# Moving the start of one-core buffers by 32 to 96 bytes: three small buffers widened at the front of the on-chip memory

## The chip, the cores and the metric

The kernel runs on one core of a Trainium2 chip. The metric is the device time of one execution in microseconds (us). Three runs of the kernel before gave 1700.7, 1705.86 and 1712.12 us; the median is 1705.86 us. The engines are named as in the profile: PE is TensorE (with PEld for its weight loads), DVE is VectorE, ACT is ScalarE, POOL is GpSimd, SP is SyncE, which here only issues transfers.

## The reference

Two transformer blocks are applied to one sequence of 256 tokens with 1024 features, all in float32. Cut to what matters:

```
first_block:  mod = silu(c) @ w_ada + b_ada                 # 1024 x 6144
              h = norm(x)*(1+scale1)+shift1 ; proj = h @ w_in
              attention over the 64 best keys of each query (chosen by an index score), short convolution
              x += gate1 * (mix @ w_out)
              h2 = norm(x)*(1+scale2)+shift2
              x += gate2 * peer_ffn(h2)
peer_ffn:     for each token: 8 heads x 16 experts of 16384 are chosen by product keys
              a = gelu(u[expert] . h2) ; sum of g*a * v[expert]    # u and v rows of 1024 floats
second_block: two feed-forwards of width 2816, retention with a context of 256 tokens,
              a Fourier branch, merge, final norm                  # weights of 1024 x 5632, 2816 x 1024, ...
```

The weights are much larger than the data: 538.50 MB pass through the DMA engines in one execution. About half of that is the expert rows: 256 tokens x 128 experts x 8 KB.

## The kernel before

**Memory.** Everything on the chip lies in buffers of 128 partitions. The helper `sb(name, width)` in `program` takes `width` words of 4 bytes from each partition, and buffers are laid one behind another in the order of the calls; the allocator starts each on a multiple of 32 bytes. In the compiled program the starts are, in bytes within a partition:

```
buffer      start    width in bytes   start modulo 64
ring        16512    65536            0
x_t         82048     8192            0
h_t         90240     8192            0
prm         98432      968            0
early       99424     3200            32
ones       102624      512            32
mod1       103136      192            32
mod2       103328      576            32
cols       103904      544            32
silu       104448      528            0
rstd       104992     1024            32
arena      106016   110592            32
small      216608    10336            32
ids        226944     1024            0
idx_stage  227968       64            0
found      228032     1024            0
spare      229056      128            0
```

**What lies where.** `ring` has four homes (slots 0 to 3) of 16 KB per partition for weight slabs. `arena` is 27648 words: two more homes for slabs (`extra`, at words 11264 and 23552), the eight buffers `rows` for expert rows (8 KB per partition each, from word 11264), homes of early modulation slabs (`spare_slab`), and most of the activations. `small` has activations and tables; its first 2048 words hold the upper half (`h_hi`) of the split activations, while the lower half (`h_lo`) is `h_t` read as float32r. `prm` has the small parameters, `early` constants, `cols` and `silu` columns of scales and of the modulation's input. `ids` has the chosen experts' numbers, `idx_stage` the 16 of them that are being fetched. `twin` gives a buffer a second name for float32r (`arena_r`, `small_r`, `h_t_r`, `ring_r`); `extra_float` and `upper` are names for parts of `arena`.

**Order of the work.** Each engine has its own written-out list, and semaphores tie the lists.
- SP (L1308 to L1364) loads `prm`, `x_t`, and then slab after slab in the order of `slab_order`, each as soon as its home is free (L1350); spare slabs of the modulation go to `arena` (L1313).
- POOL fetches expert rows. `one_round` (L1389 to L1405) copies 8 numbers from `ids` to `idx_stage` (L1395) and issues one indirect transfer for each (L1402), as soon as `row_open` finds one of the 8 buffers `rows` free. One transfer brings a row of 8 KB to each of 128 partitions.
- DVE takes the dot product of each fetched row (L2527, in `dot_batch`). The second half of the row is summed for the first 128 tokens by PE with diagonal weights (matmuls that read `small,arena`), for the last 128 tokens by DVE (L2538, in `sum_batch`) but for the last batches; after that the buffer is free.
- In the same stage PE does the context's feed-forward, with weights from `ring`. In the second block each weight piece is split in two float32r parts, the upper by ACT (L1455), the lower by DVE (L2016), and PE does three products of each; L518 is PE's matmul helper `mm`.

Of the kernel before, what the change touches and what calls it, by code (L numbers as in the profile page):

```python
# [90 lines left out]
def offsets(table):  # L91
    at, out = 0, {}
    for name, width in table:
        out[name] = (at, width)
        at += width
    return out, at


PARAM_AT, PARAM_W = offsets(PARAMS)
# [123 lines left out]
def program(nc, dram, out):  # L223
# [14 lines left out]
    with ExitStack() as ctx:  # L238
        def sb(name, width, dt=F32):
            return ctx.enter_context(nc.sbuf_tensor(name, [P, width], dt))  # L240
# [8 lines left out]
        def sem(name):  # L249
            if name not in sems:  # L250
                sems[name] = ctx.enter_context(nc.semaphore(name))
            return sems[name]
# [3 lines left out]
        x_t = sb("x_t", KD * L)[:].rearrange("p (k t) -> p k t", k=KD)  # L256
        h_words, h_words_r = twin("h_t", KD * L)
        h_t, h_lo = (t[:].rearrange("p (k t) -> p k t", k=KD) for t in (h_words, h_words_r))
        prm = sb("prm", PARAM_W)
        early = sb("early", EARLY_W)  # L260
        place = nc.alloc_sbuf_tensor_at("place", [P, SLOTS], U32, offset=nc.sbuf_base - 4 * EARLY_W + 4 * EARLY_AT["causal"][0])
        ones = sb("ones", P)
        mod1 = sb("mod1", 48)
        mod2 = sb("mod2", 144)
        mod2_v = mod2[:].rearrange("p (m k s) -> p m k s", m=9, s=2)
        cols = sb("cols", 136)
        silu = sb("silu", 132)
        rstd = sb("rstd", L)
        arena, arena_r = twin("arena", 27648)

# [148 lines left out]
        def home_of(n, ring_of):  # L419

            slot, words = slots[n][0], slabs[n][2]
            if slot >= RING:
                return extra[slot - RING][0 if ring_of is ring else 1][:, 0:words]
            return ring_of[:, slot * SLAB:slot * SLAB + words]
# [31 lines left out]
        def emptied(name):  # L456

            _, who, count = groups[index[name]]
            return drained[who], count
# [7 lines left out]
        def _(pe):  # L467
# [157 lines left out]
            def pair_by_block(o, need, hi, lo, name, order):  # L625

                two = [next_piece(j) for j in range(2)]
                for n, k in enumerate(order):
                    if k in need:
                        pe.wait_ge(*need.pop(k))  # L630
                    last = [three(o[:, j * L:(j + 1) * L], w_hi[:, k, :], w_lo[:, k, :], hi(k), lo[:, k, :],
                                  n == j == 0, n == KD - 1 and j == 1) for j, (_, w_hi, w_lo) in enumerate(two)]
                piece_end(last[0])
                piece_end(last[1], name)

            def split_feature(tag, count, hi, lo, who, kb=KD, need=None, start=0, order=range(KD)):


                need = need or {}
                for n in range(start, start + count):  # L640
                    o = begin(f"{tag}{n}", who)
                    if len(need) == KD and kb == KD:
                        pair_by_block(o, need, hi, lo, f"{tag}{n}", order)
                        continue
                    for j in range(2):
                        for part in range(kb // KD):
                            (k0, k1, _, _), w_hi, w_lo = next_piece()
                            for k in range(k0, k1):
                                if k in need:
                                    pe.wait_ge(*need.pop(k))  # L650
                                last = three(o[:, j * L:(j + 1) * L], w_hi[:, k - k0, :], w_lo[:, k - k0, :],
                                             hi(k), lo[:, k, :], k == 0, k == kb - 1)
                            ends = j == 1 and part == kb // KD - 1
                            piece_end(last, f"{tag}{n}" if ends else None)
# [653 lines left out]
        @block.sync  # L1308
        def _(sp):
            def load_spare(m):  # L1310

                home = SPARE_HOME[m][0]
                sp.dma_start(spare_slab[home], dram["w_ada_2"][MODS[m][1]]).then_inc(sem(f"spare_landed{home}"), 16)  # L1313

            sp.dma_start(prm[:], dram["params"]).then_inc(sem("params"), 16)
            sp.dma_start(x_t.rearrange("p k t -> p (k t)"), dram["x"]).then_inc(sem("x_landed"), 16)
            for n, (name, i, words) in enumerate(slabs):
                slot, _, replaced = slots[n]
                if slabs[n][:2] == ("w_ada", 5):
                    sp.wait_ge(group_done, index["ss_n1"] + 1)  # L1320
                    load_spare(12)
                if slabs[n][:2] == ("peer_wq", 1):
                    sp.wait_ge(*spare_read[12])
                    load_spare(14)
                    sp.wait_ge(*piece_read[first_pieces - 1])
                    sp.dma_start(subkeys.rearrange("p h n -> p (h n)"), dram["subkeys"][0]).then_inc(sem("subkeys"), 16)
                    sp.wait_ge(group_done, index["pt0_1"] + 1)
                    load_spare(15)
                if slabs[n][:2] == ("peer_wq", 2):
                    sp.wait_ge(sem("y_conv"), 1)  # L1330
                    sp.wait_ge(group_done, index["pv3"] + 1)
                    load_spare(16)
                    load_spare(17)
                    sp.wait_ge(*spare_read[14])
                    load_spare(19)
                    sp.wait_ge(*spare_read[15])
                    load_spare(18)
                    sp.wait_ge(*spare_read[16])
                    load_spare(20)
                if replaced is not None:  # L1340
                    sp.wait_ge(*slab_free[replaced])
                if slabs[n][:2] == MODS[LAST_ROWS[0]]:
                    sp.wait_ge(group_done, index["pr3"] + 1)
                if n == tail_at:
                    sp.wait_ge(row_landed[GBUF - 2], 16 * (NT * SLOTS // GBUF))
                if slot == RING and replaced is None:
                    sp.wait_ge(sem("row_free_dve"), GBUF + SLOTS - GBUF + 2)
                if slot == RING + 1 and replaced is None:
                    sp.wait_ge(group_done, index["yt1_1"] + 1)
                sp.dma_start(home_of(n, ring), dram[name][i]).then_inc(landed[slot], 16)  # L1350
                if n == 0:
                    sp.dma_start(early[:], dram["early"]).then_inc(sem("early_landed"), 16)
                if n == tail_at + LATE_AFTER:
                    sp.wait_ge(sem("experts_added"), 1)
                    at = 0
                    for dst, w, s in ((late_decay, LATE_DECAY, "p m t i -> p (m t i)"), (dft, LATE_DFT, "p a s c -> p (a s c)"),
                                      (rope, LATE_ROPE, "p a t -> p (a t)"), (late_xi, LATE_XI, "p a t -> p (a t)")):
                        sp.dma_start(dst.rearrange(s), dram["late"][:, at:at + w]).then_inc(sem("late"), 16)
                        at += w
            for i in range(2):  # L1360
                sp.wait_ge(sem("out_ready"), i + 1)
                sp.dma_start(out[:, 4 * i * L:(4 * i + 4) * L],
                             h_t[:, 4 * i:4 * i + 4, :].rearrange("p k t -> p (k t)")).then_inc(sem("stored"), 16)
            sp.wait_ge(sem("stored"), 16 * 2)  # L1364
# [1395 lines left out]
```

## Time and profile before

| what | value |
|---|---|
| median of 3 runs | 1705.86 us |
| the profiled execution, its own time | 1705.73 us |
| its span in the trace | 1703.8 us |
| instructions | 29036 |
| PE busy | 1627.5 us (96%) |
| DVE busy | 1167.1 us (68%) |
| ACT busy | 660.5 us (39%) |
| POOL busy | 389.6 us (23%) |
| moved by DMA | 538.50 MB, mean 316 GB/s |
| granted PE clock, mean | 0.987 |

The span is the time between the first and the last instruction of the profile; the device time of the same execution is 1.9 us longer. A busy share is an average over stages: PE counts as busy also where a matmul waits for its operands, and DMA is full in one part of the span and half idle in another, so the slices and windows have to be read and not the mean.

### The profile page before, as it was taken

How to read it: one execution, taken by the hardware profiler on the slowest of the kernel's cores; microseconds unless marked ns; L12 is line 12 of the kernel's file. 1: busy time of each engine (PE TensorE's matmuls, PEld its weight loads, DVE VectorE, ACT ScalarE, POOL GpSimd, SP SyncE). 2: the span in 40 equal slices, each digit the busy share in tenths (PEclk: the TensorE clock that was granted, in tenths of full speed). 3: DMA queues.
4: the chain of work that ended last, by engine and by line, in shares of the span. 5: the costliest groups of instructions: out<-in, count | busy, mean ns of one | idle time of the engine just before them, and what ended most of it. 6: DMA issues, size and time to landing. Idle time of an engine off the chain costs nothing.

```text
span 1703.8 us, 29036 instructions
## 1 busy us (share of the span) xinstructions
PE 1627.5 (96%) x11656; PEld 1464.0 (86%) x11656; DVE 1167.1 (68%) x1989; ACT 660.5 (39%) x1272; POOL 389.6 (23%) x317
## 2 busy tenths in 40 slices
PE   5999999988899899999998999999999999999997
PEld 3877889988899799998988567889998977989997
DVE  3675458778997677889788688564575456665554
ACT  3534133324433543433112158444434423444443
POOL 0553034434444434445343310000000000000000
PEclk9999999999999999999999999999999999999999
DMA  9868899999999999999999999865444522644442
GB/s 369 323 264 369 357 413 408 412 419 399 413 410 392 419 393 414 415 420 420 420 411 414 421 414 404 317 239 212 165 172 187 198 99 99 228 183 183 183 170 93
DMA packets 57732, 538.50 MB, mean 316 GB/s; under 512 B 6401, under 2 KB 6529, under 8 KB 7425
## 3 DMA queue, kind: packets, MB, share of 16 engines
q1 hardware_dynamic: 20592, 267.18, 39.5%
q0 software_dynamic: 37008, 269.50, 38.6%
q8 instruction: 92, 1.51, 0.4%
q14 instruction: 40, 0.32, 0.0%
HBM read 535.60 MB, written 1.05 MB: 315 GB/s over the span
## 4 chain that ended last, share of the span: by engine, by line
PE 62%; DMA 19%; DVE 10%; issue 6%; ACT 1%; POOL 1%; POOLq 0%; DVEq 0%; SPq 0%; ACTq 0%
PE psum L518 62%; DMA arena<-in_experts,idx_stage 16%; DVE arena L2538 4%; DVE arena L2527 1%; DMA ring<-in_w_ada 1%; POOL arena L1402 1%; DMA ring<-in_w_in 1%; DMA arena<-in_w_ada 1%; DMA extra_float<-in_w_ada 1%; DVE ring_r L2016 0%; POOL idx_stage L1395 0%; DVE arena L2649 0%; DVE small L2527 0%; DVE arena_r L2082 0%; ACT h_t L1832 0%
## 5 line engine op out<-in xcount | busy, mean ns | idle before, releaser
L2527 DVE CUSTOM_DVE_ANT_0 arena<-arena 128x1024 f32<-128x1024 f32 x256 | 313.8, 1226 | 133.5 <-DMA arena<-in_experts,idx_stage 127.4
L1402 POOL DMA_INDIRECT arena<-in_experts,idx_stage x256 | 303.8, 1187 | 365.7 <-DVE arena L2538 164.9
L2016 DVE TENSOR_TENSOR ring_r<-ring,ring_r 128x1024 fp32r<-128x1024 f32 (+1 forms) x200 | 240.7, 1214 | 197.0 <-ACT ring_r L1455 196.0
L518 PE MATMUL psum<-small_r,ring_r 128*128 128x256 f32 x1600 | 285.9, 283 | 3.4 <-DVE h_t_r L2097 3.4
L1455 ACT ACTIVATE ring_r<-ring 128x1024 fp32r<-128x1024 f32 (+1 forms) x200 | 208.2, 1048 | 170.4 <-PE psum L518 150.2
L518 PE MATMUL psum<-small,arena 128*128 128x128 f32 x2112 | 251.4, 280 | 22.0 <-ACT small L1858 21.7
L518 PEld LDWEIGHTS psum<-small,arena 128*128 128x128 f32 x2112 | 246.1, 196 | 25.9 <-ACT small L1858 23.0
L518 PEld LDWEIGHTS psum<-small_r,ring_r 128*128 128x128 f32 x1600 | 245.3, 189 | 5.4 <-issue 5.2
L518 PE MATMUL psum<-h_t,ring 128*128 128x256 f32 (+1 forms) x1360 | 248.1, 341 | 1.2 <-DMA ring<-in_w_in 1.2
L518 PEld LDWEIGHTS psum<-h_t,ring 128*128 128x128 f32 x1360 | 219.3, 191 | 21.9 <-DMA ring<-in_w_in 1.4
L518 PE MATMUL psum<-h_t_r,ring_r 128*128 128x256 f32 x800 | 223.8, 280 | 0.0
L518 PE MATMUL psum<-arena_r,ring_r 128*128 128x256 f32 x1488 | 211.6, 284 | 2.8 <-DVE arena_r L2082 2.8
L1920 ACT ACTIVATE small<-small 128x2 f32<-128x2 f32 x127 | 25.8, 203 | 463.9 <-DVE small L2527 463.8
L518 PEld LDWEIGHTS psum<-arena_r,ring_r 128*128 128x128 f32 x1488 | 192.9, 191 | 3.2 <-DVE arena_r L2082 3.2
L2538 DVE SCALAR_TENSOR_TENSOR arena<-arena,small 128x1024 f32<-128x1024 f32 x123 | 158.1, 1285 | 5.7 <-ACT small L1851 1.3
L518 PEld LDWEIGHTS psum<-h_t_r,ring_r 128*128 128x128 f32 x800 | 151.1, 189 | 0.1
L518 PE MATMUL psum<-arena,ring 128*128 128x128 f32 (+1 forms) x916 | 141.8, 316 | 0.0
L518 PEld LDWEIGHTS psum<-arena,ring 128*128 128x128 f32 x916 | 130.4, 192 | 10.7 <-issue 1.7
L518 PEld LDWEIGHTS psum<-ring 128*128 128x128 f32 x1056 | 122.9, 195 | 3.4 <-DVE ring L2478 1.9
L518 PE MATMUL psum<-ring 128*128 128x128 f32 x1056 | 123.2, 279 | 1.9 <-DVE ring L2478 1.7
L518 PE MATMUL psum<-ring_r,small_r 128*128 128x512 f32 x272 | 90.1, 399 | 0.8 <-DVE ring_r L2016 0.8
L518 PE MATMUL psum<-arena_r,upper 128*128 128x256 f32 x384 | 73.9, 295 | 9.9 <-DVE ring_r L2016 5.6
(281 smaller groups left out, 1687.6 us busy)
## 6 DMA issues: line engine op xcount, KB each, us to landing
ring<-in_w_in SPq DMA_DIRECT2D x31, 2048.0 KB, 8.6
ring<-in_w_ffn SPq DMA_DIRECT2D x29, 2048.0 KB, 11.2
ring<-in_w_ada SPq DMA_DIRECT2D x18, 2048.0 KB, 9.5
ring<-in_w_ffn SPq DMA_DIRECT2D x23, 1408.0 KB, 7.4
arena<-in_w_ada SPq DMA_DIRECT2D x8, 2048.0 KB, 16.4
ring<-in_w_out SPq DMA_DIRECT2D x4, 2048.0 KB, 9.3
ring<-in_peer_wq SPq DMA_DIRECT2D x4, 2048.0 KB, 10.3
extra_float<-in_w_ffn SPq DMA_DIRECT2D x4, 2048.0 KB, 12.5
```

The source lines that it names most:

```text
L518: return nc.tensor.matmul(o, a, b, start=first, stop=last)
L1402: nc.gpsimd.indirect_dma_start(rows[slot % GBUF], None, dram["experts"], bass.IndirectOffsetOnAxis(ap=idx_stage[:, slot:slot + 1], axis=0) ...
L1455: nc.scalar.activation(upper(i), whole(i, ring), ACT.Copy).then_inc(hi_made, 1)
L1920: nc.scalar.activation(acts[:, n % 8, :], dots[:, n % 8, :], ACT.Gelu_apprx_tanh).then_inc(sem("gelus"), 1)
L2016: nc.vector.tensor_tensor(whole(i, ring_r), whole(i, ring), upper(i).bitcast(F32), ALU.subtract).then_inc(lo_made, 1)
L2527: step(nc.vector.tensor_tensor_reduce(u, u, h2[:, n // PER_TILE, :], 1.0, 0.0, ALU.mult, ALU.add, dots[:, n % 8, s:s + 1]), sem("dots"))
L2538: ins = STT(y_sum, row, weight, y_sum, ALU.mult, ALU.add)
```

## The change

`prm` is widened from 242 to 256 words, `cols` from 136 to 144, `silu` from 132 to 144. The load of `prm` names its first 242 words, so it moves what it moved before. Every other instruction stays and addresses the same words of the same buffers, whose starts are now these:

```
buffer      start    modulo 64      moved by
early       99456    0              32
ones ... cols        0              32
silu       104512    0              64
rstd       105088    0              96
arena      106112    0              96
small      216704    0              96
ids        227040    32             96
idx_stage  228064    32             96
found      228128    32             96
spare      229152    32             96
```

`ring`, `x_t`, `h_t` and `prm` keep their starts. `small` is 2584 words, 161.5 times 64 bytes, so the four buffers behind it come to lie between two multiples of 64.

```
-        prm = sb("prm", PARAM_W)
+        prm = sb("prm", PARAM_W + -PARAM_W % 16)
         early = sb("early", EARLY_W)
...
-        cols = sb("cols", 136)
-        silu = sb("silu", 132)
+        cols = sb("cols", 144)
+        silu = sb("silu", 144)
         rstd = sb("rstd", L)
         arena, arena_r = twin("arena", 27648)
...
-            sp.dma_start(prm[:], dram["params"]).then_inc(sem("params"), 16)
+            sp.dma_start(prm[:, 0:PARAM_W], dram["params"]).then_inc(sem("params"), 16)
```

## Rows read from the trace of the kernel before

**Rows 1.** The page's slices of the span: clock, DMA share and rate.

```profile
PEclk9999999999999999999999999999999999999999
DMA  9868899999999999999999999865444522644442
GB/s 369 323 264 369 357 413 408 412 419 399 413 410 392 419 393 414 415 420 420 420 411 414 421 414 404 317 239 212 165 172 187 198 99 99 228 183 183 183 170 93
```

**Rows 2.** The page's chain that ended last, by engine.

```profile
PE 62%; DMA 19%; DVE 10%; issue 6%; ACT 1%; POOL 1%; POOLq 0%; DVEq 0%; SPq 0%; ACTq 0%
```

**Rows 3.** Who waited for whom: us in total, times, longest us.

```profile
POOL arena L1402 <- DVE arena L2538: 164.9, 45, 12.2
...
POOL arena L1402 <- PE psum L518: 133.3, 71, 10.2
DVE arena L2527 <- DMA arena<-in_experts,idx_stage: 127.4, 80, 6.2
```

**Rows 4.** Windows: stretch, us, each engine's busy us, clock, DMA share, GB/s.

```profile
5.00:30.00 25.00, 15.03 (x74) 10.62 (x75) 13.05 (x32) 11.43 (x15) 0.00 (x0) 0.88 1.01 432
7.00:19.00 12.00, 10.21 (x48) 5.85 (x48) 4.88 (x18) 4.29 (x6) 0.00 (x0) 1.00 1.00 427
110.00:115.00 5.00, 5.00 (x49) 4.86 (x49) 0.19 (x1) 0.00 (x0) 1.44 (x1) 1.00 1.00 423
...
178.00:200.00 22.00, 22.00 (x195) 18.89 (x194) 5.95 (x17) 5.08 (x14) 0.00 (x0) 1.00 1.01 427
213.00:1005.00 792.00, 757.09 (x5185) 689.84 (x5185) 631.69 (x1212) 259.76 (x705) 328.33 (x288) 0.98 1.00 412
937.00:980.00 43.00, 43.00 (x123) 23.24 (x122) 28.48 (x36) 6.30 (x23) 15.49 (x14) 1.00 1.01 422
```

**Rows 5.** SP's queue in time: start us, us, transfers issued in a row.

```profile
3.87 12.92 SPq L1350 DMA_DIRECT2D ring<-in_w_ada  x2
18.93 0.33 SPq L1350 DMA_DIRECT2D ring<-in_w_idx  x1
...
105.15 0.33 SPq L1350 DMA_DIRECT2D ring<-in_w_in  x1
...
166.47 25.21 SPq L1313 DMA_DIRECT2D arena<-in_w_ada  x5
```

**Rows 6.** The page's DMA issues: KB each, median us from issue to landing.

```profile
ring<-in_w_ada SPq DMA_DIRECT2D x18, 2048.0 KB, 9.5
...
arena<-in_w_ada SPq DMA_DIRECT2D x8, 2048.0 KB, 16.4
```

**Rows 7.** DVE and ACT, groups by form: busy us, mean ns, idle before.

```profile
L2016 DVE TENSOR_TENSOR ring_r<-ring,ring_r 128x1024 fp32r<-128x1024 f32 x192 | 233.1, 1224 | 188.2 <-ACT ring_r L1455 187.1
...
L2016 DVE TENSOR_TENSOR extra_float32r<-extra_float,ring_r 128x1024 fp32r<-128x1024 f32 x16 | 19.3, 1223 | 2.0 <-ACT ring_r L1455 1.9
...
L2082 DVE TENSOR_TENSOR arena_r<-arena,arena_r 128x1024 fp32r<-128x1024 f32 x4 | 4.9, 1224 | 1.3 <-ACT arena_r L1977 1.2
```

**Rows 8.** PE, groups by form, same columns.

```profile
L518 PE MATMUL psum<-small_r,ring_r 128*128 128x256 f32 x1600 | 285.9, 283 | 3.4 <-DVE h_t_r L2097 3.4
L518 PE MATMUL psum<-h_t,ring 128*128 128x256 f32 x848 | 186.5, 380 | 1.2 <-DMA ring<-in_w_in 1.2
L518 PE MATMUL psum<-arena,ring 128*128 128x256 f32 x352 | 77.4, 380 | 0.0
```

**Rows 9.** PE matmuls of 1500 to 1690 us by tile: min/median/max ns.

```profile
L518 PE MATMUL psum<-small_r,ring_r x704: 275/282/375, 1506.3 to 1631.8; 128*128 128x256 f32 x176
L518 PE MATMUL psum<-arena_r,ring_r x495: 277/280/283, 1632.0 to 1689.9; 128*128 128x256 f32 x165
L518 PE MATMUL psum<-h_t_r,ring_r x352: 276/277/284, 1506.4 to 1631.7; 128*128 128x256 f32 x176
```

**Rows 10.** POOL's indirect transfers and index copies by tile: min/median/max ns.

```profile
L1402 POOL DMA_INDIRECT arena<-in_experts,idx_stage x256: 932/1004/1931, 213.6 to 988.3; - x128
L1395 POOL COPY idx_stage<-ids x32: 187/924/1208, 212.4 to 966.0; 128x8 uint32 x26, 128x8 uint32<-128x8 uint32 x6
```

**Rows 11.** DVE's clearing of `silu` by tile: min/median/max ns.

```profile
L2190 DVE MEMSET silu<- x1: 168/168/168, 0.8 to 0.8; 128x132 f32 x1
```

**Rows 12.** The page's issue row of the expert rows (256 x 1 MB).

```profile
arena<-in_experts,idx_stage POOLq DMA_INDIRECT x256, 11.6
```

## The prediction

> **What bounds the kernel now.** The slices of the span come first, because the change moves addresses and nothing else, and an address can matter only where a resource that uses it is full. They show two parts [rows 1]. Up to about 213 us the DMA share wavers between 0.6 and 1; from there to about 1060 us it is full in every slice, at 392 to 421 GB/s; from 1100 us on it is mostly about half, at 93 to 240 GB/s. The clock digits show nothing but nines: PE's granted clock is near its full level of 2.4 GHz throughout, so the clock is no lever here.
>
> The chain that ended last gives PE 62%, DMA 19% and DVE 10% [rows 2]. The waits tell how DMA and DVE are tied in the full part: DVE waits 127.4 us for expert rows, and POOL waits 164.9 us for DVE's sum and 133.3 us for PE to free a row buffer [rows 3]. It is a loop over eight buffers. A transfer takes 11.6 us at the median from issue to landing [rows 12], though 1 MB at the stage's 412 GB/s [rows 4] needs only 2.5 us: the rest is queueing, so POOL's and SP's issues are well ahead of the engines that move the bytes. From 213 to 1005 us the windows have DMA at 1.00 and PE busy for 757 of 792 us. So a faster or slower DMA write to `arena` would show there, and a slower PE read would show everywhere else.
>
> **The change part by part.** It removes no instruction and adds none. Three questions of cost are left, one for each kind of access, and one small term.
>
> *The clearing of `silu`* covers 144 words in place of 132. The memset took 168 ns for 132 [rows 11]; 12 more at 168/132 = 1.3 ns each are at most 15 ns. It runs at 0.8 us, when DVE would otherwise wait for the first loads. Without that cover it would cost the 15 ns. I take 0. The load of `prm` moves the same 242 words to the same place: 0.
>
> *DMA writes to `arena`* (all 256 MB of expert rows, 16 MB of early modulation slabs, the `extra` slabs) start 32 bytes past a multiple of 64 now and will start on one. The trace holds both kinds side by side, since `ring` and `x_t` already start on multiples of 64. From 7 to 19 us the queue carries the slabs issued to `ring` and the early small loads [rows 5], at 427 GB/s and share 1.00; from 178 to 200 us it carries modulation slabs to `arena`, at 427 GB/s and share 1.01 [rows 4]. A second stretch with `ring` alone, 110 to 115 us, behind the issue at 105.15, has 423. The same size of row, the same queue, the same rate: the start makes no difference that this trace can show. One row seems to speak the other way: a modulation slab takes 9.5 us to land in `ring` and 16.4 us in `arena` [rows 6]. But five of the eight `arena` slabs were issued close together, from 166.47 to 191.7 us [rows 5], and at 427 GB/s each needs 2.1 MB / 427 = 4.9 us, so 16.4 us is the time to stand behind two others and not a slower write. Value taken: 0. The ends: a gain if `arena` in the full part (422 GB/s in its quietest window) rose to the best `ring` window, 432 [rows 4], 2.3% of 792 us = 18 us; a loss if it fell from 427 to the worst, 423, 0.9% of 792 us = 7 us. Both are too large even so, as part of those 792 us is bounded by PE.
>
> The Trainium skill ("DMA: Bandwidth & Descriptors", How a descriptor splits into AXI transactions) knows no step at 64 bytes but one at 256: a transfer that starts off such a boundary pays for the bytes below its start. It speaks against this change, for by the addresses a row starts 32 past a boundary before and 128 past it after: 8 + 248 + 1 = 257 beats against 8 + 248 + 4 = 260. By that rule my sum would be 1.2% of the full part, +9 us, an estimate from the page. The trace does not agree, since `ring`, which lies 128 past a boundary, would have to be slower than `arena`, and the two windows above are equal.
>
> *DVE and ACT* work on both kinds of addresses in the same operation. The lower part of a piece of 128x1024 takes 1224 ns in `ring`, 1223 ns in `extra` and 1224 ns from `arena` to `arena` [rows 7]. Value 0; the end is 1 ns x 256 dot products, 0.3 us, on either side.
>
> *PE* reads its moving operand from `h_t` or from `arena`: 380 ns both, over 848 and 352 matmuls [rows 8]. In float32r one pair differs: 282 ns at the median from `small_r` (off 64) and 277 from `h_t_r` (on 64) [rows 9]. This looks like a price of the address. But in the second feed-forward's other half both parts come from `arena_r`, off 64 all of them, and yet their times span 277 to 283 ns with a median of 280. A third of the matmuls takes the lower part there too. So the 5 ns go with the place in the triple of products, not with the buffer. Value 0. The end, if the address were the cause: 5 ns x 1600 matmuls [rows 8] = 8 us of gain, and about as much again for `arena_r` at half the difference or less; I put 12 us.
>
> *`ids` and `idx_stage`* lose the multiple of 64. POOL's issue of an indirect transfer takes 932 ns at least and 1004 at the median, the copy of 8 numbers 924 [rows 10]. The numbers in slots 8 to 15 of `idx_stage` lie 32 bytes on already, and half of the 256 issues use them; the median is only 72 ns above the least. If every issue paid 72 ns more it would be 18 us on POOL, which is busy for 328 of the stage's 792 us [rows 4] and whose issues land 11.6 us later from queueing. The queue's depth hides it; without that cover it would be the 18 us. Value 0.
>
> **The sum** is 0 against the profiled execution, 1705.73 us, a span of 1703.8 and 1.9 us around it. The median of the runs, 1705.86, is 0.1 us above it. The three runs lie 11 us apart (0.7%), which is why I take 1% as the least that can be told from no change. Forecast 1705.
>
> **The rivals.** *Faster: the write to an aligned `arena` is quicker.* For it: the full part has 412 GB/s on average and 422 at its quietest, `ring` alone reached 432. Against it: the 427 and 427 of the direct comparison, and that the full part's writes are mixed with instruction and index traffic. Gain 9 us (422 to 427) to 18 us (to 432), so 1688 to 1697. Chance 9%.
>
> *Faster: PE's reads.* The 5 ns of above, a gain of about 12 us, 1694. Against it the spread of the `arena_r` matmuls. Chance 3%.
>
> *Slower: rows that start 128 past a boundary of 256.* It decides in the full part, where DMA is at 1.00, and only while DMA's rate and not PE sets the pace. Priced from rows it is the step from 427 to 423 GB/s, 7 us, time 1713. For it: the second `ring` window. Against it: the first. Chance 7%. The page's rule named above would make it 9 us.
>
> *The change does not do what it says.* The four buffers of indices end up off the 64, and something there matters: POOL's fetch, which reads one number per partition from `idx_stage`. It would need the buffers' loop to run short of issues: up to 18 us, 1724; partly hidden, 1710. Chance 3%.
>
> **How the numbers follow.** The forecast has 78%. Of the two gains, 12% together, 7 points exceed 1% (17 us) when I allow that a price can be larger than the rows' ends; of the two losses, 10%, 5 points do. The same: 100 - 7 - 5 = 88%. The range reaches from 1694, where the gains are at their middle, to 1715, past the loss from the 256 boundary, and includes the 1701 to 1712 of the kernel's own scatter.
>
> **What would show it.** Equal instruction counts and the same chain. In windows with DMA at 1.00 between 213 and 1005 us, the rate stays near 412 GB/s, and the last expert row is issued within a few us of 988 [rows 10]. The writes' rival would show a stage that ends some 9 to 18 us earlier at a higher rate; PE's rival, `small_r` matmuls at 277 ns; the 256 rival, 5 GB/s less in the windows of slabs to `arena`; the index rival, POOL's least time above 932 ns. I am wrong if DMA gains in the mixed traffic what it does not show in the lone stretches.

## The result, and the profile after

The change makes the kernel slower by a little: 1711.23 us median against 1705.30, a ratio of 1.0034 with a 95% interval of 1.0023 to 1.0045. The profiled execution has a span of 1709.4 us against 1703.8, so the trace holds 5.6 us of it. The order of the instructions is the same on every engine, 29036 of them; the one shape that differs is that of the clearing of `silu`, 128x144 for 128x132.

The page after, its busy times:

```profile
PE 1633.1 (96%) x11656; PEld 1470.1 (86%) x11656; DVE 1170.0 (68%) x1989; ACT 660.2 (39%) x1272; POOL 386.8 (23%) x317
```

PE is busy for 1633.1 us, 5.6 more than before. The windows of the changed kernel (columns as in [rows 4]), three of those of [rows 4] first, then three in the second block:

```profile
7.00:19.00 12.00, 9.52 (x44) 5.85 (x48) 4.89 (x18) 5.07 (x5) 0.00 (x0) 1.00 1.00 427
...
178.00:200.00 22.00, 22.00 (x195) 18.89 (x194) 5.95 (x17) 4.64 (x13) 0.00 (x0) 1.00 1.01 429
213.00:1005.00 792.00, 758.17 (x5195) 689.21 (x5188) 632.58 (x1219) 260.52 (x706) 325.20 (x289) 0.99 1.00 412
...
1240.00:1275.00 35.00, 35.00 (x294) 35.00 (x293) 26.00 (x33) 13.47 (x14) 0.00 (x0) 1.00 0.48 181
...
1510.00:1620.00 110.00, 110.00 (x918) 109.94 (x917) 61.06 (x65) 52.12 (x62) 0.00 (x0) 1.00 0.49 186
1640.00:1685.00 45.00, 45.00 (x378) 45.00 (x377) 24.53 (x28) 20.85 (x30) 0.00 (x0) 1.00 0.48 174
```

The same three windows of the kernel before:

```profile
1240.00:1275.00 35.00, 35.00 (x300) 35.00 (x299) 26.60 (x33) 13.20 (x13) 0.00 (x0) 1.00 0.48 181
...
1510.00:1620.00 110.00, 110.00 (x936) 109.97 (x935) 61.23 (x62) 53.07 (x62) 0.00 (x0) 1.00 0.49 186
1640.00:1685.00 45.00, 45.00 (x386) 45.00 (x385) 23.57 (x27) 21.96 (x30) 0.00 (x0) 1.00 0.44 161
```

The first thing to see is what did not move. The expert rows' stage runs at 412 GB/s before and after, the slabs to `arena` at 427 and 429. POOL's indirect transfers end where they ended (compare [rows 10]):

```profile
L1402 POOL DMA_INDIRECT arena<-in_experts,idx_stage x256: 932/1060/1978, 214.9 to 988.7; - x128
```

The last is issued at 988.7 us for 988.3. So at most 0.4 us of the 5.6 come from the part in which DMA is full; the rest comes after it.

The second thing is the count beside PE. In the second block's windows PE is busy for the whole of them, before and after, and its share says nothing. But fewer matmuls fit: 918 for 936, 378 for 386, 294 for 300. A matmul lasts some 280 ns by its record and overlaps its neighbours, so a window counts also those that started up to 0.28 us before it, and the pace, the time from the start of one matmul to the start of the next, is (window + 0.28) / count: 110.28/936 = 117.8 ns before, 110.28/918 = 120.1 after; 45.28/386 = 117.3 before, 45.28/378 = 119.8 after. The durations show it only weakly, 283 to 284 ns for `small_r` (compare [rows 8]):

```profile
L518 PE MATMUL psum<-small_r,ring_r 128*128 128x256 f32 x1600 | 290.2, 284 | 3.4 <-DVE h_t_r L2097 3.4
L518 PE MATMUL psum<-h_t_r,ring_r 128*128 128x256 f32 x800 | 226.5, 283 | 0.0
L518 PE MATMUL psum<-arena_r,ring_r 128*128 128x256 f32 x1488 | 214.5, 286 | 2.7 <-DVE arena_r L2082 2.7
```

The same groups had busy times of 285.9, 223.8 and 211.6 us before, so these three grew by 9.9 us; others shrank: the 272 matmuls with 512 columns from `ring_r` against `small_r` from 90.1 to 89.1, those within `ring` from 123.2 to 121.8, those from `small,arena` from 251.4 to 250.6. The row of `h_t_r` is the telling one: `h_t` and `ring` have not moved by a byte, and its matmuls are slower all the same.

### The profile page after: what moved, and what is told of

It reads as the page before. It is cut to its first block, busy times and chain, and to the rows that moved or that the text cites. A ratio compares the mean times of both kernels' runs of the same rounds, so it can differ in the third digit from the quotient of the medians.

```text
span 1709.4 us, 29036 instructions
## 1 busy us (share of the span) xinstructions
PE 1633.1 (96%) x11656; PEld 1470.1 (86%) x11656; DVE 1170.0 (68%) x1989; ACT 660.2 (39%) x1272; POOL 386.8 (23%) x317
## 4 chain that ended last, share of the span: by engine, by line
PE 61%; DMA 19%; DVE 10%; issue 6%; ACT 2%; POOL 1%; POOLq 0%; DVEq 0%; SPq 0%; ACTq 0%
PE psum L518 61%; DMA arena<-in_experts,idx_stage 16%; DVE arena L2538 4%; DVE arena L2527 1%; DMA ring<-in_w_ada 1%; DMA ring<-in_w_in 1%; POOL arena L1402 1%; DMA arena<-in_w_ada 1%; DMA extra_float<-in_w_ada 1%; DVE ring_r L2016 0%; DVE small L2527 0%; DVE arena L2649 0%; DVE arena_r L2082 0%; ACT h_t L1832 0%; ACT L1920 0%
## 5 line engine op out<-in xcount | busy, mean ns | idle before, releaser
L2527 DVE CUSTOM_DVE_ANT_0 arena<-arena 128x1024 f32<-128x1024 f32 x256 | 313.8, 1226 | 133.5 <-DMA arena<-in_experts,idx_stage 127.2
L518 PE MATMUL psum<-small_r,ring_r 128*128 128x256 f32 x1600 | 290.2, 284 | 3.4 <-DVE h_t_r L2097 3.4
L518 PE MATMUL psum<-small,arena 128*128 128x128 f32 x2112 | 250.6, 279 | 20.8 <-ACT small L1858 20.6
L518 PEld LDWEIGHTS psum<-small_r,ring_r 128*128 128x128 f32 x1600 | 250.6, 192 | 5.5 <-issue 5.2
L518 PE MATMUL psum<-ring 128*128 128x128 f32 x1056 | 121.8, 277 | 1.6 <-DVE ring L2478 1.6
L518 PE MATMUL psum<-ring_r,small_r 128*128 128x512 f32 x272 | 89.1, 395 | 0.8 <-DVE ring_r L2016 0.8
```

The source lines that it names most:

```text
L518: return nc.tensor.matmul(o, a, b, start=first, stop=last)
L2527: step(nc.vector.tensor_tensor_reduce(u, u, h2[:, n // PER_TILE, :], 1.0, 0.0, ALU.mult, ALU.add, dots[:, n % 8, s:s + 1]), sem("dots"))
```

## The experiments

All experiments on the full kernel change the layout of the memory alone, except two at the end. The quantity that they turned out to be about is the distance from the start of `ring` (weights) to the start of `arena` or `small` (moving operand), modulo 256 bytes: 160 before (106016 - 16512 = 89504 = 349 x 256 + 160), 0 after (89600 = 350 x 256). `h_t` is at 0 in both. The first four expectations name a window of 42.6 us (364 matmuls before, 357 after); the two windows from 1510 and from 1640 us, each in one kind of work, have taken its place. Each kernel was timed against the kernel before on the same chip.

**Arena, and what lies behind it, moved by 32 bytes** (`small` and the index buffers move with it).

```
         rstd = sb("rstd", L)
+        gap = sb("gap", 8)
```

> The kernel before with one unused buffer of 8 words put between rstd and arena: arena and small move by 32 bytes onto a multiple of 64, ids to spare move with them off it, everything in front of them stays. Theory PE: a float32r matmul of 256 columns paces at 120 ns when its moving operand lies on a multiple of 64 (or at the same place in 64 as the weights) and at 117 ns when it lies 32 bytes off; the whole slowdown of the change comes from arena and small. It expects 1711 us, and 357 matmuls in a window of 42.6 us filled with them (364 before). Theory front: the slowdown comes from the small buffers in front (cols, silu, early, rstd): 1705 us and 364. Theory DMA (rows further behind a boundary of 256 bytes cost more; arena is now 64 behind one, 32 before the change, 128 after it): a third of the loss, 1707 us, with 364 matmuls in the window.

Measured: 1701.32 us, ratio 0.9974 (0.9959 to 0.9990). Faster, where one theory had 1711, another 1705, the third 1707. `arena` lies on a multiple of 64 here as in the changed kernel, and the pace of the matmuls from it is the quickest seen, 45.28/399 = 113.5 ns. So 64 is not the rule. The distance is 192. The index buffers lie off a multiple of 64 here as in the changed kernel, and the kernel is faster all the same: they are not the cause either.

```profile
1510.00:1620.00 110.00, 110.00 (x925) 110.00 (x924) 60.26 (x59) 51.91 (x60) 0.00 (x0) 1.00 0.49 186
1640.00:1685.00 45.00, 45.00 (x399) 45.00 (x398) 24.90 (x30) 22.08 (x30) 0.00 (x0) 1.00 0.45 161
```

**The changed kernel with the same gap** (distance 32).

> The changed kernel with the same unused buffer of 8 words between rstd and arena: the front stays on multiples of 64, arena and small go back to 32 bytes off (160 behind a boundary of 256). Theory PE: the loss is gone, 1705 us, 364 matmuls in the window. Theory front: 1711 us, 357. Theory DMA: at 160 behind a boundary no better than at 128, 1711 us or more, with 364 in the window.

Measured: 1704.26 us, ratio 0.9991 (0.9977 to 1.0005), 388 matmuls in the last window and 935 in the one before. The loss is gone with the front buffers still moved: it does not come from them, and it is not DMA's.

**Everything of the changed kernel moved by 32 bytes**, with one line ahead of `ring`:

```
+        shift = sb("shift", 8)
         ring, ring_r = twin("ring", RING * SLAB)
```

> The changed kernel with an unused buffer of 8 words in front of ring: every buffer of the change moves by 32 bytes, so the weights in ring and the moving operands in small, arena and h_t are all 32 off a multiple of 64. Two forms of theory PE part here. Absolute: the moving operand's own place in 64 counts; all are off, so 1705 us or a little less and 364 or more in the window. Relative: what counts is whether moving operand and weights lie at the same place in 64; they do, so 1711 us and 357.

Measured: 1709.06 us, ratio 1.0021 (1.0008 to 1.0034), still slow. `ring`, `h_t`, `arena` and `small` all lie 32 off a multiple of 64 now, and PE paces as in the changed kernel (the profiled execution took 1705.68 us):

```profile
1640.00:1685.00 45.00, 45.00 (x377) 45.00 (x377) 23.23 (x27) 21.25 (x29) 0.00 (x0) 1.00 0.42 158
```

The relative form of the theory holds: the distance counts, the place does not. This kernel and the one above it are the sharpest pair here: `arena`, `small` and the index buffers start at the same addresses in both (`arena` at 106144), and only `ring` and what lies between it and `arena` start 32 bytes further in this one. They take 1709.06 and 1704.26 us, so neither DMA's writes to `arena` nor the index buffers can be what separates them.

**The kernel before with the same line ahead of ring** (distance 160 again, `arena` on a multiple of 64).

> The kernel before with an unused buffer of 8 words in front of ring: ring and h_t come to lie 32 off a multiple of 64, arena and small on one. Weights and moving operands are 32 apart for arena and small, as before the change, but with the roles exchanged. Absolute: arena and small on 64 pace at 120 ns, so about 1710 us. Relative: 1705 us, 364 in the window.

Measured: 1705.39 us, ratio 0.9994 (0.9981 to 1.0008), as the relative form has it. The windows have 927 and 382, 118.9 and 118.5 ns, between before and after, where 936 and 386 were expected. The distance of 160 has two paces in these kernels, and the kernel before shows both by itself: from `arena`, 171 matmuls in the window from 1435 to 1455 us (20.28/171 = 118.6 ns) and the 386 of the last window (117.3).

**PE alone.** The kernel has the second block's pattern of matmuls on zeros, no other engine at work:

```
for k in range(3):
    mm(o, w_hi[k], hi[k]); mm(o, w_hi[k], lo[k]); mm(o, w_lo[k], hi[k])
```

> This kernel computes nothing of the reference: PE alone runs matmuls in the second block's pattern (of three, the first two with the same weights, the third with others; 256 columns of float32r) on zeros, 144 from each of 14 buffers that start 0, 16, 32, 48, 64, 80, 96, 112, 128, 160, 192, 224, 256 and again 0 bytes behind the weights modulo 1024 (mova to movn in that order); then 48 each with 512 columns of the weights' buffer as moving operand and stationary buffers at 0, 32, 64, 96 (stata, statc, state, statg); then 72 each in plain float32 at 0, 32, 64, 96 (plaina, ...). No other engine works. Theory distance: PE reads the moving operand and the next weights at the same time and is held up by where they lie to each other; the pace goes with the distance modulo 128: 120 ns at 0, 117 at 32, 113 at 64, about 117 at 96, 120 again at 128 and 256, and 113 at 192. Rival, traffic: the distance only shifts how PE meets the reads and writes of ACT and DVE; with no other engine at work all buffers give the same pace. Rival, bus of 64: 0, 64, 128, 192 alike, and 32 apart from them.

The windows of 15 us, one in each block, in the order of the distances 0, 16, 32, 48, 64, 80, 96, 112, 128, 160, 192, 224, 256, 0 (columns: PE, PEld, DVE, POOL):

```profile
39.00:54.00 15.00, 15.00 (x128) 15.00 (x127) 0.00 (x0) 0.00 (x0) 1.00 0.00 1
56.00:71.00 15.00, 15.00 (x129) 15.00 (x128) 0.00 (x0) 0.00 (x0) 1.00 0.00 1
73.00:88.00 15.00, 15.00 (x131) 15.00 (x130) 0.00 (x0) 0.00 (x0) 1.00 0.00 1
90.00:105.00 15.00, 15.00 (x129) 15.00 (x128) 0.00 (x0) 0.00 (x0) 1.00 0.00 1
107.00:122.00 15.00, 15.00 (x129) 15.00 (x129) 0.00 (x0) 0.00 (x0) 1.00 0.01 1
124.00:139.00 15.00, 15.00 (x127) 15.00 (x126) 0.00 (x0) 0.00 (x0) 1.00 0.00 1
142.00:157.00 15.00, 15.00 (x127) 15.00 (x126) 0.00 (x0) 0.00 (x0) 1.00 0.00 1
159.00:174.00 15.00, 15.00 (x135) 15.00 (x134) 0.00 (x0) 0.00 (x0) 1.00 0.00 1
175.00:190.00 15.00, 15.00 (x129) 15.00 (x128) 0.00 (x0) 0.00 (x0) 1.00 0.00 1
192.00:207.00 15.00, 15.00 (x131) 15.00 (x130) 0.00 (x0) 0.00 (x0) 1.00 0.00 1
208.50:223.50 15.00, 15.00 (x135) 15.00 (x134) 0.00 (x0) 0.00 (x0) 1.00 0.00 1
225.00:240.00 15.00, 15.00 (x130) 15.00 (x129) 0.00 (x0) 0.00 (x0) 1.00 0.00 1
242.00:257.00 15.00, 15.00 (x127) 15.00 (x126) 0.00 (x0) 0.00 (x0) 1.00 0.01 1
259.50:274.50 15.00, 15.00 (x127) 15.00 (x126) 0.00 (x0) 0.00 (x0) 1.00 0.01 1
```

With 15.28 us over the counts: about 120 ns at 0 and 256, 117 at 32 and 160, 118 at 16, 48, 64, 128 and 224, 120 at 80 and 96, 113 at 112 and 192; one matmul more or less in a window is 0.9 ns. The clock is 1.00, and DVE, ACT and POOL do nothing, so the theory of traffic falls. Of the curve expected only 0, 32, 192 and 256 came out: 128 is not slow, and 96 and 64 are not what they were to be. At 128 the pace of 0 does not come back, at 256 it does, so 256 is the shortest period that fits. Most distances were seen once, in one order, and later runs show that one distance can have two paces: a value between 113 and 119 is a pace of that distance and perhaps not its only one. The matmuls in plain float32 did not care: 94 and 95 records in windows of 20 us at the distances 0 and 96 (the profile has two records for each of them).

**Everything at 64**, with `step_64 = sb("step_64", 16)` behind `ring` and a gap of 24 words before `arena`.

> The kernel before with an unused buffer of 16 words behind ring and one of 24 words before arena: h_t, arena and small all start 64 bytes behind ring modulo 128 (before the change h_t 0, arena and small 32). Theory distance: all float32r matmuls of 256 columns pace at 113.4 ns, as those from arena did with the gap of 32 bytes; against before that is 2.4 ns on 800 matmuls from h_t, 6.7 on 1600 from small, 2.5 on 1488 from arena, 16 us in all: 1689 us, and 970 matmuls in the window from 1510 to 1620 us (936 before, 925 with the gap of 32). Rival: only arena's reads profit, and h_t with small stays at 118 ns: 1701 us and 930. Rival, traffic: no rule of distance holds; anywhere from 1700 to 1711.

Measured: 1703.75 us, ratio 0.9991 (0.9976 to 1.0005), 936 and 384 in the windows: 1689 was wrong. The value for 64 had been taken from the kernel at 192, with the wrong period. PE alone has 118 ns at 64, and 45.28/384 = 117.9 agrees.

**Arena at 224**, a gap of 16 words.

> The kernel before with an unused buffer of 16 words before arena: arena and small start 96 bytes behind ring modulo 128. Theory distance, if it is even about 64: the pace of the matmuls from arena is again 117 ns, 385 in the window from 1640 to 1685 us, and the time 1705 us. If it falls steadily with the distance to 128: 110 ns and 1697 us. If it repeats at 64: 385 and 1705 too.

Measured: 1704.35 us, ratio 0.9990 (0.9973 to 1.0006), 383 in the window, 118.2 ns; PE alone has 130 in 15 us at 224, 117.5 ns, the same within one matmul.

**Arena at 0, the front as before**, a gap of 24 words.

> The kernel before with an unused buffer of 24 words before arena: arena and small start a multiple of 128 bytes (and of 512) behind ring, as in the changed kernel, and everything in front of them lies as before. Theory distance: 1711 us, 378 matmuls in the window from 1640 to 1685 us and 918 from 1510 to 1620: the whole loss of the change with none of its small buffers moved. Theory front: 1705 us.

Measured: 1710.68 us, ratio 1.0034 (1.0015 to 1.0052), the change's own ratio to the last digit, with 919 and 377 matmuls in the windows (918 and 378 in the changed kernel). None of the change's three buffers is widened here, and `arena` and `small` start at the changed kernel's very addresses. This is the change's whole effect without the moves in front of `arena`. The index buffers move here too, but the kernel with the gap of 8 words has cleared them.

**Mixed distances, PE alone.** The upper and the lower part of the moving operand come from buffers at different distances.

> This kernel computes nothing of the reference: PE alone, as in the first one of this kind, but with the upper and lower parts of the moving operand in buffers at different distances behind the weights: upper 160, 192, 32, 224 with lower 0, then upper 0 with lower 192; 144 matmuls each. Theory distance, if the pace is PE's own also for mixed places: the averages of the full kernels from h_t and small: 117.9 ns at 160 and 0, 119.3 at 192 and 0, 117.9 at 32 and 0, 117.8 at 224 and 0. Then weights and moving operands all 32 bytes further (32 and 32: 120.0 ns; 32 and 224: 113.4 ns, as 0 and 192), since only the distance counts. Then 512 columns from the weights' buffer with the stationary operand at 0, 160, 192, 224, 64: 227 at 0 and 231 to 234 at the others. Rival, traffic: the mixed paces in the full kernels came from ACT and DVE, and here they are plain means of the pure ones (for 192 and 0: 115.6).

Windows in the blocks of upper 160, 192, 32, 224 with lower 0, then 0 with 192, then weights and moving operands 32 bytes further at distances 0 and 192:

```profile
32.00:47.00 15.00, 15.00 (x130) 15.00 (x129) 0.00 (x0) 0.00 (x0) 1.00 0.00 1
48.50:63.50 15.00, 15.00 (x128) 15.00 (x127) 0.00 (x0) 0.00 (x0) 1.00 0.00 1
65.50:80.50 15.00, 15.00 (x130) 15.00 (x129) 0.00 (x0) 0.00 (x0) 1.00 0.00 1
82.50:97.50 15.00, 15.00 (x130) 15.00 (x128) 0.00 (x0) 0.00 (x0) 1.00 0.01 1
99.50:114.50 15.00, 15.00 (x130) 15.00 (x129) 0.00 (x0) 0.00 (x0) 1.00 0.01 1
116.50:131.50 15.00, 15.00 (x128) 15.00 (x127) 0.00 (x0) 0.00 (x0) 1.00 0.01 1
133.50:148.50 15.00, 15.00 (x135) 15.00 (x134) 0.00 (x0) 0.00 (x0) 1.00 0.00 1
```

That is 117.5 ns for 160 and 0 (the kernel before: 117.8) and 119.4 for 192 and 0 (the kernel with the gap of 8: 110.28/925 = 119.2). The plain mean of the pure paces, 115.6 for 192 and 0, which the theory of traffic expected, did not come. It explains the row of `h_t_r`: a lower part that has not moved is paced together with an upper part that has. The last two repeat 120 and 113 at the shifted place. The matmuls with 512 columns go the other way, slightly: 41 in 9 us with the stationary operand at 0, 40 at 160, 41 at 192, 40 at 224 and 64.

**Everything at 192.** `mod1`, 192 bytes, is put behind `ring` and a gap of 8 words before `arena`; beside it ran the kernel with the gap of 8 words again.

```
+        mod1 = sb("mod1", 48)
         x_t = sb("x_t", KD * L)[:].rearrange("p (k t) -> p k t", k=KD)
...
-        mod1 = sb("mod1", 48)
...
         rstd = sb("rstd", L)
+        gap = sb("gap", 8)
```

> The kernel before with mod1 (192 bytes) laid right behind ring instead of behind ones, and an unused buffer of 8 words before arena: h_t, arena and small all start 192 bytes behind ring modulo 256 (h_t 0, arena and small 160 before the change). Theory distance, now with the period of 256 bytes that the kernel with PE alone gave: every float32r matmul of 256 columns paces at 113.4 ns, 970 in the window from 1510 to 1620 us (936 before) and 397 from 1640 to 1685 (386 before); 16 us less than before, 1689 us, if ACT and DVE keep up with the splitting. Rival: the splitting by ACT and DVE becomes the bound; then the windows of 5 us show PE waiting for DVE ring_r, and the time stays near the 1701 of the kernel with arena alone at 192.

> The kernel before with the gap of 8 words before arena once more, beside the one with everything at 192: h_t 0, arena and small 192 behind ring modulo 256. Theory distance: 1701 us as in its first run, 12 us above the one with everything at 192, and 399 matmuls in the window from 1640 to 1685 us. Rival, chance: if its first 1701 was luck of the chip it will be 1705.

Measured: 1702.41 us, ratio 0.9984 (0.9969 to 0.9998), and 1701.76, ratio 0.9978 (0.9962 to 0.9994). The gap's gain stands; of the 16 us for everything at 192 only 3 came. In the second profile of the gap kernel the window from 1510 us has 937 matmuls (110.28/937 = 117.7 ns), where the first had 925 (119.2): the same kernel, on another chip, has run the same stretch at two paces.

```profile
1510.00:1620.00 110.00, 110.00 (x937) 110.00 (x936) 61.72 (x61) 52.02 (x61) 0.00 (x0) 1.00 0.51 189
```

The windows with everything at 192 show why the rest did not come, and it is not ACT and DVE, since PE is busy throughout:

```profile
1510.00:1620.00 110.00, 110.00 (x938) 110.00 (x937) 61.62 (x61) 51.70 (x61) 0.00 (x0) 1.00 0.51 192
1640.00:1685.00 45.00, 45.00 (x385) 45.00 (x384) 24.01 (x29) 20.05 (x28) 0.00 (x0) 1.00 0.37 137
```

385 matmuls, 117.6 ns, from an `arena` at the very address at which the gap kernel makes 400 (113.2 ns) of the same instructions. Distance alone does not set the pace.

**What ran before a block, PE alone.** Blocks from a buffer at 192, each after something else; beside it the kernel with everything at 192 once more.

> This kernel computes nothing of the reference: PE alone, blocks of 108 matmuls. The buffer atlast is 192 bytes behind the weights modulo 256, atzero 0, atsixty 64, athundred 160, twin 192 (the lower part's buffer in two blocks). A block from atlast follows each of: atzero, atsixty, athundred, a block of mixed distances, three pauses in which PE waits for DVE, float32r matmuls with 512 columns, plain float32 matmuls. Theory history: at 192 PE has two stable patterns, 113.4 and 117.8 ns, and what ran before a block sets which it falls into; some blocks from atlast show the one and some the other, each throughout the block. Rival, traffic: in the full kernel the 117.8 came from the accesses of ACT and DVE; here every block from atlast shows 113.4. At 0 both expect 120.0.

> The kernel with everything at 192 once more, one look. Theory history, if the order of instructions alone sets the pattern: the same stretches at 113.4 and 117.8 ns as in its first profile, 385 matmuls in the window from 1640 to 1685 us and 938 from 1510 to 1620. If the times of the waits set it, which differ from run to run: other stretches, 385 or 397 in the one window and anything from 935 to 970 in the other.

Windows in blocks at 192 that follow a block at 160, a block of mixed distances, and the 24 matmuls with 512 columns:

```profile
76.00:85.00 9.00, 9.00 (x82) 9.00 (x81) 0.00 (x0) 0.00 (x0) 1.00 0.01 2
99.00:110.00 11.00, 11.00 (x99) 11.00 (x98) 0.00 (x0) 0.00 (x0) 1.00 0.01 1
...
211.00:222.00 11.00, 11.00 (x96) 11.00 (x95) 0.00 (x0) 0.00 (x0) 1.00 0.00 1
```

9.28/82 = 113.2 and 11.28/99 = 113.9, against 11.28/96 = 117.5 ns, with nothing but PE at work: two stable patterns at one distance. Of all the blocks at 192 only two ran slowly, the one after the 512 columns and the one after plain float32; pauses in which PE waited for DVE left the pattern quick. The full kernel took 1701.98 us and had 937 and 385 in these windows, as before. But a stretch of 6 us from 1507 has 53 matmuls, where the first profile has 56 (118.5 and 112.1 ns), and the gap kernel's two profiles differ in more. So the order of the work fixes the pattern in most stretches and not in all; the times of the waits and the chip also differed, and nothing here tells these two apart.

**One extra matmul.** Eighteen blocks at 192, nine after 512 columns and nine after plain float32, with one or a few matmuls of another kind between.

> This kernel computes nothing of the reference: PE alone. Eighteen blocks of 72 matmuls from atlast (192 behind the weights modulo 256), nine of them each right after 24 matmuls with 512 columns, then nine each right after 36 plain float32 matmuls; between these and the block stand, in order: nothing, 1 matmul from atzero, 3 from atzero, 1 from athundred (160), 1 from atsixty (64), 1 from atlast with 64 columns, 1 with 128, 1 with 192, 1 from atzero with 64. Theory history: the pattern is set at the block's start by how the reads of moving operand and weights stand to each other, so the first of each nine shows 117.8 ns and some of the others 113.4, each for its whole block. Rival: the 512 columns or the plain float32 set a mode of PE that stays until a pause; then all eighteen show 117.8.

Windows of 7 us. After 512 columns, with between: nothing, 1 from distance 0, 3 from distance 0, 1 from distance 64, 1 with 64 columns, 1 with 128. After plain float32: nothing, 1 from distance 0, 1 with 64 columns, 1 with 128:

```profile
29.50:36.50 7.00, 7.00 (x62) 7.00 (x61) 0.00 (x0) 0.00 (x0) 1.00 0.00 0
43.50:50.50 7.00, 7.00 (x61) 7.00 (x61) 0.00 (x0) 0.00 (x0) 1.00 0.00 0
58.00:65.00 7.00, 7.00 (x64) 7.00 (x63) 0.00 (x0) 0.00 (x0) 1.00 0.01 2
85.40:92.40 7.00, 7.00 (x65) 7.00 (x64) 0.00 (x0) 0.00 (x0) 1.00 0.01 2
99.20:106.20 7.00, 7.00 (x64) 7.00 (x63) 0.00 (x0) 0.00 (x0) 1.00 0.00 0
113.00:120.00 7.00, 7.00 (x62) 7.00 (x61) 0.00 (x0) 0.00 (x0) 1.00 0.00 0
...
164.50:171.50 7.00, 7.00 (x62) 7.00 (x61) 0.00 (x0) 0.00 (x0) 1.00 0.01 2
188.50:195.50 7.00, 7.00 (x64) 7.00 (x63) 0.00 (x0) 0.00 (x0) 1.00 0.01 2
284.40:291.40 7.00, 7.00 (x62) 7.00 (x61) 0.00 (x0) 0.00 (x0) 1.00 0.00 0
308.30:315.30 7.00, 7.00 (x64) 7.00 (x63) 0.00 (x0) 0.00 (x0) 1.00 0.00 0
```

61 or 62 matmuls are the slow pattern (7.28/62 = 117.4 ns), 64 or 65 the quick one (113.8). One matmul that takes a tenth of a microsecond decides over the whole block of 72 behind it, and not by a simple rule: with 64 columns it gives the quick pattern after 512 columns and the slow one after plain float32, with 128 the other way round. A mode that stays until a pause is ruled out.

**The extra matmul in the full kernel**, everything at 192:

```
+            def nudge(o, w_hi, a_hi):
+                mm(o[:, 0:128], w_hi, a_hi[:, 0:128], True, True)
...
+                                if n == start and j == k == 0:
+                                    nudge(o, w_hi[:, 0, :], hi(0))
```

(and at the start of both parts of the last feed-forward; with 64 for 128 in the first of the two kernels).

> The kernel with everything at 192 (1702.41 us median), with one extra float32r matmul of 64 columns at the start of each run of weight pieces of the second block and of the first block's w_in (some 25 of them; the real ones write over what it leaves). Theory history: the extra matmul moves some stretches from 117.8 to 113.4 ns; if all of the second block moved, 970 matmuls in the window from 1510 to 1620 us and 397 from 1640 to 1685, and 1689 to 1692 us. If it moves some the one way and some the other: 1695 to 1702. Rival: waits and the other engines' times set the pattern in the full kernel, the nudge makes no difference: 1702 us, 938 and 385.

> The same with extra matmuls of 128 columns. Theory history: with PE alone 64 and 128 columns gave opposite patterns after the same predecessor, so here other stretches pace at 113.4 than with 64; the time again between 1689 and 1702 us, and different from the one with 64. Rival as there: 1702 us.

Measured: 1700.64 us, ratio 0.9975 (0.9958 to 0.9991), with 64 columns; 1696.85 us, ratio 0.9948 (0.9929 to 0.9967), with 128. The second beats both kernels of this case, by 0.5% and 0.8%. Its stretch from 1640 to 1680 us has 355 matmuls, 40.28/355 = 113.5 ns, where the kernel without the extra matmuls has 342:

```profile
1510.00:1620.00 110.00, 110.00 (x937) 110.00 (x937) 62.61 (x62) 52.97 (x62) 0.00 (x0) 1.00 0.53 199
1640.00:1680.00 40.00, 40.00 (x355) 40.00 (x354) 21.47 (x26) 17.90 (x25) 0.00 (x0) 1.00 0.38 140
```

The feed-forward from `small` and `h_t` stays at 937, 117.7 ns, and no kernel here has moved it as a whole to the quick pattern; its 1056 matmuls [rows 9] at 4.4 ns would be 4.6 of the 16 us. Another stretch with the same two operands did move. From 1335 to 1355 us this kernel has 179 matmuls, 20.28/179 = 113.3 ns, and the one without the extra matmuls 173, 117.2 ns:

```profile
1335.00:1355.00 20.00, 20.00 (x179) 20.00 (x178) 9.05 (x8) 9.38 (x11) 0.00 (x0) 1.00 0.55 211
```

Other stretches went the other way: from 1435 to 1450 us, from `arena`, 129 for 135. With 64 columns the time can't be told from that of the kernel without extra matmuls (the intervals 0.9958 to 0.9991 and 0.9969 to 0.9998 overlap); with 128 it can.

## Why the prediction was wrong

*DMA writes, value 0*: right. The rates are 412 and 412, 427 and 429, and the kernel with a gap of 24 words, nothing in front of `arena` moved, reproduces the whole loss with its last expert row issued at 988.4 us, 988.3 before. The Trainium skill ("DMA: Bandwidth & Descriptors", How a descriptor splits into AXI transactions) would have had 9 us from the boundary of 256 bytes, by the prediction's estimate from its rule, with the right sign and a size not far off. It is not the cause: the stage in which DMA is full has not become longer (last issue 988.7 for 988.3 us), and of two kernels with `arena` at the same 160 bytes behind such a boundary one is slow and one is not (1709.06 and 1704.26 us).

*POOL's index buffers, value 0*: right in effect. The least time stayed at 932 ns; the median rose from 1004 to 1060, and DVE waited 127.2 us for expert rows, 127.4 before.

*DVE and ACT, `silu`, `prm`, value 0*: right.

*PE, value 0, with a gain of 12 us as the end*: this is the step that failed. It asked only whether a buffer lies on a multiple of 64, and settled it by durations: 277 to 283 ns within `arena_r`, so "the 5 ns go with the place in the triple of products, not with the buffer". Two things were wrong there. The measure was one: records of 277 to 283 ns overlap, and what costs time is the pace from start to start, which is (window + 0.28) / count and stood in the same trace. The other was the inference. The place in the triple is the same in the changed kernel, and there the 5 ns are gone, 283 ns for both, with `h_t` where it was:

```profile
L518 PE MATMUL psum<-small_r,ring_r x607: 278/283/366, 1509.7 to 1619.9; 128*128 128x256 f32 x152
L518 PE MATMUL psum<-h_t_r,ring_r x303: 274/283/284, 1509.9 to 1619.7; 128*128 128x256 f32 x152
```

The 5 ns went with `small` at 160 and `h_t` at 0 from `ring`, and so with the buffers after all: what counts is how the moving operand lies to the weights modulo 256 bytes. The change brought that distance from 160 to 0, where the pace is 120 ns and not 117 to 119. At 2.3 ns on 2400 matmuls from `small` and `h_t` and 2.5 ns on 1488 from `arena` that would be 9 us, an estimate from two windows and a high one, since other stretches lost half as much: from 1335 to 1370 us the windows have 297 and 294, 118.8 and 120.0 ns. PE's busy time rose by 5.6 us. The sign was wrong too: the range allowed this step a gain and no loss, because 64-byte alignment was taken for the only thing that could matter.

*The slower rival* had the right sign with the wrong mechanism and place. *The range*, 1694 to 1715, holds 1711; *the forecast* of no change within 1% holds, and its direction, none, does not: the loss of 0.34% is clear of the scatter.

## What to carry to other kernels

Where PE is busy throughout, its share can't show a loss; count the matmuls in a window of fixed length and divide. When buffers move in memory, ask how the operands that PE reads lie to each other, not whether each is aligned: a moving operand at the same place modulo 256 bytes as the weights cost 2% of the pace here, and padding for alignment brought exactly that about. A layout is worth a sweep with PE alone, and the result is worth checking in the full kernel, since the same distance, and even the same kernel, can run a stretch at two paces.

## What the runs showed of the hardware that was not expected

- The pace of float32r matmuls with 256 columns goes with the distance of moving operand and weights, modulo 256 as far as tried: 120 ns at 0 and 256 wherever they were measured (changed kernel, 0 with everything shifted, 0 by a gap, four blocks with PE alone), between 113 and 120 elsewhere. Plain float32 shows no such thing. The Trainium skill ("SBUF — State Buffer", Who interferes with whom) counts two independent read ports for PE, one for the moving operand and one for weights. The runs with PE alone don't fit full independence: the pace changed with nothing but the distance of the two. That the two reads get into each other's way is inferred; no run here separates them.
- At a distance of 192 there are two patterns, 113.4 and 117.8 ns, each stable for a whole block of 72 or 108 matmuls, with PE alone. What ran just before sets it there, and one extra matmul can change it. At 160 the kernel before shows 117.3 and 118.6 ns from `arena` in one profile. In the full kernel the same program has shown both patterns in one stretch (937 and 925 matmuls, 56 and 53), so there something beside the order of the work has a say. What rule picks the pattern stays open, and with it why the last feed-forward never reached 113 as a whole.
- DMA wrote at the same rate to starts 32 and 0 past a multiple of 64 bytes, 427 and 429 GB/s.
